# A hybrid conv/gMLP block on eight cores: where the row, weight and store transfers of the mixing phase are issued

## The reference, cut to what matters

```python
def reference(x, ...):                      # x: (4, 8192, 1024) float32
    h = rmsnorm(x, norm1_g)
    p = h @ w_in                            # 2560 columns: B, C, x~ | u, v
    y_a = b_gate * causal_depthwise_conv(c_gate * xc, conv_w)     # width 3
    y_b = u * spatial_gating(layernorm(v, ...), gmlp_ws, gmlp_bs) # 128x128 per head
    y = concat([rmsnorm(y_a, g_a), rmsnorm(y_b, g_b)])
    x = x + y @ w_out                       # 1024 x 1024
    a = relu(rmsnorm(x, norm2_g) @ w_up)    # 1024 -> 4096
    x = x + (a * a) @ w_down                # 4096 -> 1024
    return rmsnorm(x, final_g)
```

## Time and profile before

| | us |
|---|---|
| median of 3 runs | 1343.01 |
| lowest and highest of them | 1251.41, 1452.58 |
| the profiled execution, its time | 1261.22 |
| its span (core 7, the slowest) | 1259.7 |
| spans of the eight cores | 1229.1 to 1259.7 |
| TensorE busy in that span | 1193.1 (95%) |
| VectorE, ScalarE, GpSimd busy | 884.7, 602.8, 58.0 |

### The profile page before, as it was taken

How to read it: one execution, slowest core, us unless ns; L and a number is a source line. 1 busy time by engine, 2 the same in 40 slices (tenths; PEclk the granted TensorE clock), 3 DMA queues, 4 the chain that set the end, 5 groups by cost and what they waited for, 6 DMA issues and landing times.

```text
span 1259.7 us, 18690 instructions; the slowest of 8 cores (1229.1 to 1259.7 us)
## 1 busy us (share of the span) xinstructions
PE 1193.1 (95%) x5784; PEld 539.6 (43%) x5784; DVE 884.7 (70%) x1346; ACT 602.8 (48%) x1141; POOL 58.0 (5%) x93
## 2 busy tenths in 40 slices
PE   6999959994999999999979999999999999999997
PEld 3444424442444444444434444444444444444443
DVE  4987837872686798737858835797844796853786
ACT  4566636563556647426307623616623606632614
POOL 0001000000000000020000001000001000001000
PEclk9999979997999999999989999999999999999999
DMA  9988785887744576799996428866527786527723
GB/s 278 286 236 231 231 142 143 207 229 71 201 87 131 163 211 212 147 188 263 190 198 212 177 90 211 208 149 220 194 87 188 212 143 205 218 76 184 223 36 134
DMA packets 101185, 227.08 MB, mean 180 GB/s; under 512 B 59744, under 2 KB 59872, under 8 KB 96224
## 3 DMA queue, kind: packets, MB, share of 16 engines
q1 hardware_dynamic: 85456, 170.83, 45.1%
q0 software_dynamic: 11024, 46.67, 21.8%
q10 hardware_dynamic: 4608, 8.39, 2.2%
HBM read 174.48 MB, written 65.01 MB: 190 GB/s over the span
## 4 chain that ended last, share of the span: by engine, by line
PE 83%; DMA 12%; SPq 1%; DVE 1%; issue 1%; ACT 1%; DVEq 0%; ACTq 0%; POOLq 0%
PE PS L515 83%; DMA HT<-HTK 3%; DMA h_s<-HTK 2%; DMA RU<-wup 2%; DMA wsu_s<-RU 2%; SPq L602 1%; DMA STC<-wcxb 1%; DMA STG<-wu 1%; DMA X<-xT 1%; DMA STG<-wv 1%; ACT SQ L522 0%; ACT HTK L522 0%; SPq L542 0%; DVE RB L534 0%; ACT VH L522 0%
## 5 line engine op out<-in xcount | busy, mean ns | idle before, releaser
L515 PE MATMUL PS<-RD,A 128*128 128x512 f16 x1792 | 392.4, 380 | 8.5 <-DVE RD L531 8.5
L515 PE MATMUL PS<-H,RU 128*128 128x512 f16 x1792 | 391.8, 379 | 1.2 <-DVE SN L531 1.2
L515 PEld LDWEIGHTS PS<-RD,A 128*128 128x128 bf16 x1792 | 175.8, 98 | 221.8 <-issue 12.1
L515 PEld LDWEIGHTS PS<-H,RU 128*128 128x128 f16 x1792 | 175.2, 98 | 213.2 <-issue 2.4
L522 ACT ACTIVATE SN<-PS 128x512 f32<-128x512 f32 x256 | 150.3, 594 | 172.6 <-PE PS L515 168.8
L515 PE MATMUL PS<-HT,WCXB 128*128 128x512 f16 x768 | 173.0, 379 | 1.5 <-DVE HT L531 1.5
L531 DVE TENSOR_TENSOR SN<-PS,SN 128x512 f32<-128x512 f32 x192 | 130.4, 688 | 62.5 <-PE PS L515 43.7
L531 DVE TENSOR_TENSOR RB<-PS,RB 128x512 f32<-128x512 f32 x96 | 65.9, 689 | 113.3 <-PE PS L515 112.7
L515 PEld LDWEIGHTS PS<-HT,WCXB 128*128 128x128 f16 x768 | 74.4, 98 | 91.5 <-issue 2.9
L515 PE MATMUL PS<-WO,YN 128*128 128x512 f16 x448 | 103.2, 379 | 1.8 <-DVE X L531 1.5
L531 DVE TENSOR_TENSOR A<-A 128x512 bf16<-128x512 bf16 (+1 forms) x192 | 94.8, 509 | 10.1 <-ACT A L522 3.7
(11 more groups left out here) (95 smaller groups left out, 860.2 us busy)
## 6 DMA issues: line engine op xcount, KB each, us to landing
RU<-wsu_s SPq DMA_DIRECT2D x56, 896.0 KB, 5.3
RD<-wsd_s SPq DMA_DIRECT2D x32, 1024.0 KB, 5.9
x_s<-X SPq DMA_DIRECT2D x32, 512.0 KB, 3.2
X<-xN POOLq DMA_DIRECT2D x20, 512.0 KB, 10.4
h_s<-HTK ACTq DMA_DIRECT2D x32, 256.0 KB, 6.1
wsd_s<-wdn POOLq DMA_DIRECT2D x16, 512.0 KB, 8.1
RA<-x_s POOLq DMA_DIRECT2D x16, 512.0 KB, 8.5
RB<-x_s POOLq DMA_DIRECT2D x16, 512.0 KB, 6.7
```

The lines of the kernel that those rows point to most:

```text
L515: ins = e.matmul(real(o_), lhsT=l, rhs=r, start=st, stop=sp, skip_group_check=True)
```

## The change

- HTK has seven buffers: three for rows that are transposed, four for rows that are stored. PREP has one buffer.
- `half_some` and `prep_some` go. `early(m)`, called at the end of pass m after `load_x(m+3)`, issues the operations of `EARLY[m]` in order ("p" a `prep`, "h" a `half`): "ph" in passes 1 and 3, "php" in 2 and 4, "phhh" in 5 and 6. Each waits for the landed store of row block 1 of the pass (`("x1", m, 1)`).
- `half` is described as two pieces of 2048 values by 64 rows, the piece outermost, on both sides; each has a semaphore of its own, and a planner weight of 2.0 for 1.7.
- Transposing DMAs have a planner weight of 0.2 for 0.7.
- In group 0, all eight `add_x1` come in p = 1: two after q = 2, two after q = 3 (RA), one after each of q = 4 to 7 (RB). The other groups keep theirs.

```diff
-        PREP = [... for i, a in enumerate((90, 97))]
+        PREP = [... for i, a in enumerate((90,))]
-        HTK = [... for i, a in enumerate((104, 106, 108, 198))]
+        HTK = [... for i, a in enumerate((104, 106, 98, 108, 198, 100, 102))]
...
         def turn(out, in_, reads, writes, dkey, nbytes, group=None, margin=1.0):
-                  nbytes=2.6 * nbytes, occ=0.6, margin=margin, packet=0.7, group=group)
+                  nbytes=2.6 * nbytes, occ=0.6, margin=margin, packet=0.2, group=group)
...
-            i = nxt("htx", 2) if x else 2 + nxt("hth", 2)
+            i = nxt("htx", 3) if x else 3 + nxt("hth", 4)
...
-        def prep(i, n):
-            combine(PREP[n], ..., (i, ("pl", n), ("ps", n)), WO.keys(3) if i < 2 else [], 5.0)
+        def prep(i, pace):
+            combine(PREP[0], ..., (i, ("pl",), ("ps",)), pace, 5.0)
...
-            dma("pool", wsd_d[p, a, 64 * h:64 * h + 64].rearrange("p q n -> p (q n)"), wdn_d[p, a, 64 * h:64 * h + 64],
-                pace, [("wd", p, a, h)], ("wh", i % 4), 4 * 64 * 4096, margin=5.0, packet=1.7)
+            dst = wsd_d[p, a, 64 * h:64 * h + 64].rearrange("p (u q) n -> u p (q n)", u=2)
+            dma("pool", dst, wdn_d[p, a, 64 * h:64 * h + 64].rearrange("p (u n) -> u p n", u=2),
+                pace, [("wd", p, a, h)], ("wh", i), 4 * 64 * 4096, margin=5.0, packet=2.0)
...
+        def early(m):
+            pace = [("x1", m, 1)]
+            for kind in EARLY[m]:
+                pos[kind] += 1
+                (prep if kind == "p" else half)(pos[kind] - 1, pace)
+
+        EARLY = ["", "ph", "php", "ph", "php", "phhh", "phhh", ""]
...
-                if c == 2:
-                    half_some(m, YA.keys(c))
...
-                if c == 2 or c == 0 and m == 2:
-                    prep_some(m)
-                if c == 3 and m in (4, 5, 6):
-                    half_some(m, YB.keys(c))
...
             if m + 3 < NMT:
                 load_x(m + 3)
+            early(m)
...
-                    if p == 1 and q % 2 == 0:
+                    if p == 1 and g > 0 and q % 2 == 0:
                         add_x1(g, 1, q // 2, [("up", q)])
+                    if p == 1 and g == 0 and q >= 2:
+                        for h, s in (((0, 0), (0, 1)), ((0, 2), (0, 3)), ((1, 0),), ((1, 1),), ((1, 2),), ((1, 3),))[q - 2]:
+                            add_x1(0, h, s, [("up", q)])
...
-                    if p == 0 and p_ in (P4, P5, P3):
+                    if p == 0 and g > 0 and p_ in (P4, P5, P3):
```

More of the change, by code:

```diff
@@ L461, in build_program @@
         XQ = [ar.buf(f"XQ{i}", (o + a) * KB, [8, MT], BF16) for i, a in enumerate((126, 90))]
-        PREP = [ar.buf(f"PREP{i}", (o + a) * KB, [7, 4, 128], F16) for i, a in enumerate((90, 97))]
+        PREP = [ar.buf(f"PREP{i}", (o + a) * KB, [7, 4, 128], F16) for i, a in enumerate((90,))]
         RS1 = [ar.buf(f"RS1{i}", (o + a) * KB, [MT], F32) for i, a in enumerate((78, 68))]
-        HTK = [ar.buf(f"HTK{i}", (o + a) * KB, [2, MT], F16) for i, a in enumerate((104, 106, 108, 198))]
+        HTK = [ar.buf(f"HTK{i}", (o + a) * KB, [2, MT], F16) for i, a in enumerate((104, 106, 98, 108, 198, 100, 102))]
         RSX = ar.buf("RSX", (o + 104) * KB, [MT], F32)
@@ L771, in combine @@
             dma("sp", dst, p[:, :, :, :], p.keys(0, 7), [("ws", i)], skey, 2 * 128 * 3584, margin=5.0, packet=1.4)
-        def prep(i, n):
-            combine(PREP[n], wsu_d[i].rearrange("p (a k n) -> p a k n", a=7, k=4),
-                    wup_d[i].rearrange("p (a k n) -> p a k n", a=4, k=4), (i, ("pl", n), ("ps", n)),
-                    WO.keys(3) if i < 2 else [], 5.0)
+        def prep(i, pace):
+            combine(PREP[0], wsu_d[i].rearrange("p (a k n) -> p a k n", a=7, k=4),
+                    wup_d[i].rearrange("p (a k n) -> p a k n", a=4, k=4), (i, ("pl",), ("ps",)), pace, 5.0)
         def half(i, pace):
             p, a, h = i // 8, (0, 1, 3, 2)[i // 2 % 4], i % 2
-            dma("pool", wsd_d[p, a, 64 * h:64 * h + 64].rearrange("p q n -> p (q n)"), wdn_d[p, a, 64 * h:64 * h + 64],
-                pace, [("wd", p, a, h)], ("wh", i % 4), 4 * 64 * 4096, margin=5.0, packet=1.7)
+            dst = wsd_d[p, a, 64 * h:64 * h + 64].rearrange("p (u q) n -> u p (q n)", u=2)
+            dma("pool", dst, wdn_d[p, a, 64 * h:64 * h + 64].rearrange("p (u n) -> u p n", u=2),
+                pace, [("wd", p, a, h)], ("wh", i), 4 * 64 * 4096, margin=5.0, packet=2.0)
         P1, P2, P3, P4, P5, P6, P7 = (0, 3), (1, 4), (6, 1), (2, 6), (4, 2), (5, 5), (3, 0)
@@ L1115, in up @@
             refill(1)
[L1117 to L1128, removed]
+        def early(m):
[4 more added lines that the diff above has]
+        EARLY = ["", "ph", "php", "ph", "php", "phhh", "phhh", ""]
+        pos["p"] = pos["h"] = 0
         for m in range(NMT):
```

## The result

The change makes the kernel slower: the ratio of its time to the time before is 1.0495, with a 95% interval of 1.0373 to 1.0617. The profiled execution took 1313.74 us with a span of 1312.2, where I had forecast 1223 in a range up to 1280. Medians here are of all executions (1320.57 after, 1301.62 before, of four each), also of disturbed ones, in which the cores of a die run at a lower clock; ratios leave those out, and g3_four, f3_pass6_free and h1_phases_best have too few undisturbed ones for a ratio.

A forecast was written before the change was run, and what follows sets the result against it. The prediction took TensorE to bound the kernel, with three holes to win back. Core 7 summed as 1261.2 - 17.2 - 18.2 - 8 + 6 = 1223.8 us; the forecast was 1223 us, range 1208 to 1280.

The forecast's parts named there:

- 4 KB pieces: Half copied in smaller packets so other queues get in between: at most 3 us per transfer meeting a half, taken as 0.
- (c): Rival, chance 0.15: a half runs on two DMA engines only, 25 us each, making the kernel slower, up to 1288 us.
- 44 + 24 + 15: Microseconds lost in (c): late x rows in four passes, second preps of passes 2 and 4, group 0's casting loads.
- Seven row buffers: Removes ScalarE's wait for the store two rows before, and so the first hole: 17.2 us gained on core 7.
- the third buffer of transposed rows: Lets VectorE write one more row ahead; VectorE's own waits for it are small, gain taken as 0.
- the first hole: TensorE idle at 157 to 189 us, on every core, from a late h2_s store; 14.4 + 2.8 us on core 7.
- the second hole: TensorE idle at 283 to 315 us, from a late transposing DMA; 15.8 + 2.4 us on core 7, none on core 4.
- Preparation behind the x rows: Moving casting loads and halves out of mid-pass removes the second hole: 18.2 us on core 7, nothing on core 4.
- my term for x rows: x rows landing close to their use in passes 1 to 4: 1.5 us each, 6 us added, ends 0 and 20.
- One PREP buffer: In passes 2 and 4 the second prep waits for the first one's store; 0 taken as likeliest, 10 us for the range.
- Group 0: Moved adds let casting loads land earlier near 630 us: -10 to +10.7 on core 7; taken as 8 there, 0 on core 4.
- The sum: All terms added from the profiled time: 1223.8 us for core 7 and 1221.0 for core 4, forecast 1223.

The follow-up runs named there:

- g3_four: Kernel after the change with the half as 4 pieces of 64 x 1024 values, piece outermost; its one profiled execution took 1250.43 us.
- f3_pass6_free: e4 with the ten halves two a pass in passes 1 to 5 and none in pass 6; 1250.86 us median, no ratio.
- h1_phases_best: e4 with halves two a pass in passes 1 to 5 and group 0's adds in their old places; 1268.41 us median, no ratio.
- e2: Kernel before the change with only the half in the new form, 2 pieces of 64 x 2048 values; 1354.63 us, ratio to before 1.0744.
- f1: e4 with four row buffers HTK again, two and two, in place of seven; 1250.39 us, ratio to before 0.9903.
- e4: Kernel after the change with the half as 128 rows of 2048 values, rows outermost; 1236.04 us, ratio to before 0.9844.
- f4: e4 with preparation and the ten halves back in the middle of a pass, still one PREP and seven row buffers; 1225.25 us, ratio to before 0.9721.
- g1: f4 with group 0's adds also in their old places; 1219.28 us, ratio to before 0.9671.
- g2: Kernel before the change with seven HTK row buffers and one PREP buffer, nothing else; 1225.31 us, ratio to before 0.9714.
- f2: e4 with group 0's accumulating DMAs in their old places; 1229.28 us, ratio to before 0.9752.
- e3: Kernel after the change with the half as 16 pieces of 64 x 256 values, piece outermost; 1235.15 us, ratio to before 0.9819.
- e1: Kernel after the change with the half described as before, 16 pieces of 16384 values; 1242.34 us, ratio to before 0.9863.

## Why the prediction was wrong

**The step that failed** is "4 KB pieces", with "I take 0". I priced the new form from the engine time of a half over sixteen engines, and kept the case of two engines as rival (c) at 0.15. It measured 78 us on the kernel after (1314 against 1236), and 7.4%, some 93 us, on the kernel before. The number in (c), 25 us for a half on two engines, was right: the smallest landings are 30.5 us in the kernel after and 22.8 in e2. What I gave as evidence against it, that halves have different engines to go to and that a late x row is late for ScalarE first, did not help: a transfer spread over sixteen engines is complete only when its packets on those two are through, and from 280 to 290 us, with the x row and the half both unfinished, only some two packets of queue 0 are in flight. The rows could not show the rule; but the piece of 2 outermost was in the diff, and nothing in the trace spoke for its staying without effect. It should have been the likeliest case.

**Where (c) was short.** It had x rows, second preparations and casting loads, at up to 44 + 24 + 15, and three of the five holes are these. It did not have the transposing DMAs: 38 us beside three halves in pass 6, and 10 at 340 us. Its 1288 was 26 us under the 1314; as those two holes are 48 us, its other terms came out smaller than priced.

**Seven row buffers.** Right, the first hole went on all cores, in the kernel after too: no wait of ScalarE ahead of a write to HTK for its store is left. Undersized: 17.2 us forecast, 34 measured for the buffers, with one PREP and the planner's new order, on the kernel before, and 14 between f1 and e4. The 0 for the third buffer of transposed rows may be the error, since the second hole went with it; that is argued only.

**Preparation behind the x rows.** No gain where I had 18.2 - 6 = 12.2 us. I took the whole 18.2 us of the second hole because core 4 had none. Against the same kernel with the old places (f4) the kernel with the new ones is 11 us slower, some of it the planner's order. Three halves in pass 6 met the first H, which my term for x rows did not hold, and what had made the second hole is gone without the move (f4, g1, g2). Whether the wait for the landed x1 store costs by itself was not tried.

**One PREP buffer.** GpSimd waited 57.7 us for its store in two waits in the kernel after, and f4, g1 and g2, which have one, are the fastest: no cost seen, as forecast.

**Group 0.** Gain taken as 8 on core 7, 0 on core 4. The kernels with the old places are 6 to 7 us faster (f2, g1), within the range of -10 to +10.7; that this is the adds and not the order is not shown.

**The sum.** Without the failing step it was 1223, and the mended kernel took 1236: the buffers did more than thought, places and adds gave nothing. Three slips changed nothing: the half's outermost dimension before was 16 and not 64; the idle time of the second hole's stretch is 3.44 us and not 3.3; and the terms of (c) add up to 100 us and not 97. One reading was too quick: the transposing DMA of 32.65 us did not land in a stretch with full DMA engines to its end, since the share is 0.15 from 300 us on the earlier trace rows.

## What to carry to other kernels

Read a DMA by its outermost dimension as issued, not by the bytes or the length of its pieces: a view that puts a dimension of 2 in front leaves two DMA engines to work and makes transfers that are spread over all of them late. A DMA share near 2/16 with compute engines idle is a hint of it, and a jump in the number of the smallest packets another; a run with the form alone undone is the proof. And when several edits are bundled, run them one by one: here the buffers alone gave 2.9%, nearly all that any of these kernels gained, one line held all of the loss, and the moved transfers showed no gain. Where a planner makes a new order for every edit, look in the profile for the wait that the edit was to remove before a difference of some 10 us is put down to it.

## What the runs showed of the hardware

- A casting copy of 512 KB from memory to memory lands at the least in 22.8 us (e2) or 30.5 us (kernel after) with 2 pieces outermost, 20.1 with 4 (g3), 7.6 with 16 (e3), and 7.8 with 128 rows (e4).
- With 2 pieces of 64 rows outermost, a copy has 896 packets of 4 bytes beside its 128 of data; with 4 pieces, 768 beside 256; with 16 pieces or 128 rows none of these.
- The transposing DMAs move in packets of 256 bytes. From 100 to 720 us, in microseconds with nothing of queue 0 in flight, they start 479 to 512 packets a microsecond (before, after, e1, e3, e4); with something of it in flight, 71 to 122, whatever the form of the copy. Why was not tried.
- In the 38 us hole the granted clock was 0.61 from 460 to 480 us, with 1.96 us of TensorE work, and 0.50 from 480 to 497 us, with none: the lower of its two levels (1.2 GHz).
```profile
480.00:497.00 17.00, 0.00 (x0) 0.00 (x0) 0.00 (x0) 0.00 (x0) 0.00 (x0) 0.50 1.39 68
```
